# Fine weight parts on GpSimd at the ends of products, last products tile by tile, second norms in another order

## What is computed

```python
def layer(x, xc, ...):                       # first block, l = 0, 1
    h = modulate(x, g_norm1, sh1, sc1)       # rms_norm(x) * (1 + scale) + shift
    proj = h @ w_in                          # keys, values, queries, Fourier part, gates
    ...                                      # two attentions and a Fourier mix
    x = x + gt1 * merge_branches(...)        # ends in "y @ w_o"
    x = x + gt2 * conv_ffn(modulate(x, g_norm2, sh2, sc2))   # w_up, conv, silu, "@ w_down"
    # xc, the context, the same way in layer 0 alone

def second_block(x, ...):
    for layer in range(2):
        y = mixer_ab(x) if layer == 0 else mixer_c(x)        # ends in "y @ w_out"
        x = layer_norm(DEEPNORM_ALPHA * x + y, ln_gain[layer], ln_bias[layer])
```

## Time and profile before

| | us |
|---|---|
| median of three runs | 2040.17 |
| lowest, highest | 2037.59, 2048.16 |
| the profiled execution | 2048.43 |
| its span | 2046.6 |
| TensorE busy | 1922.9 |
| VectorE busy | 1184.9 |
| ScalarE busy | 932.2 |
| GpSimd busy | 161.0 |

### The profile page before, as it was taken

How to read it: one execution, slowest core, us unless ns; L and a number is a source line. 1 busy time by engine, 2 the same in 40 slices (tenths; PEclk the granted TensorE clock), 3 DMA queues, 4 the chain that set the end, 5 groups by cost and what they waited for, 6 DMA issues and landing times.

```text
span 2046.6 us, 31430 instructions
## 1 busy us (share of the span) xinstructions
PE 1922.9 (94%) x12063; PEld 1624.1 (79%) x12063; DVE 1184.9 (58%) x1944; ACT 932.2 (46%) x1424; POOL 161.0 (8%) x173
## 2 busy tenths in 40 slices
PE   5999998899998999999998989989998999799997
PEld 2875666688887888888784779989988888699996
DVE  3426556533346555533545555677744568789987
ACT  3337444422225333321436555455533646387682
POOL 4010000000001222210000000013400000000000
PEclk9999999999998999999998999989999999899999
DMA  9225557444332233233250026645557433454342
GB/s 297 96 75 165 168 183 246 121 102 105 91 103 83 83 102 102 83 112 102 93 151 14 1 67 179 192 138 180 180 185 229 124 104 103 144 165 144 125 145 103
DMA packets 262824, 265.37 MB, mean 130 GB/s; under 512 B 6310, under 2 KB 230928, under 8 KB 262720
## 3 DMA queue, kind: packets, MB, share of 16 engines
q1 hardware_dynamic: 257856, 249.32, 39.1%
q0 software_dynamic: 4416, 13.49, 2.2%
q10 hardware_dynamic: 448, 1.12, 0.2%
HBM read 262.81 MB, written 1.10 MB: 129 GB/s over the span
## 4 chain that ended last, share of the span: by engine, by line
PE 76%; DVE 12%; ACT 6%; issue 3%; DMA 3%; SPq 0%; DVEq 0%; ACTq 0%
PE bank L476 20%; PE bank L477 20%; PE bank L478 20%; PE bank L694 4%; PE bank L710 4%; DVE weights_fine L1788 3%; PE bank L470 2%; PE bank L534 2%; PE bank L523 2%; DMA region<-in_w_mod 2%; ACT weights_coarse L1121 2%; PE bank L701 1%; DVE region L2392 1%; DMA region<-in_w_in_ab 1%; PE bank L943 0%
## 5 line engine op out<-in xcount | busy, mean ns | idle before, releaser
L1788 DVE TENSOR_TENSOR weights_fine<-region,weights_coarse 128x2048 fp32r<-128x2048 f32 (+3 forms) x187 | 431.5, 2308 | 377.4 <-ACT weights_coarse L1121 376.1
L1121 ACT CAST weights_coarse<-region 128x2048 fp32r<-128x2048 f32 (+3 forms) x187 | 358.8, 1918 | 353.6 <-PE bank L478 328.6
L476 PE MATMUL bank<-normed_coarse,weights_coarse 128*128 128x256 f32 (+1 forms) x1104 | 371.8, 337 | 9.7 <-DVE fourier_out_fine L1802 5.4
L477 PE MATMUL bank<-normed_fine,weights_coarse 128*128 128x256 f32 (+1 forms) x1104 | 370.9, 336 | 0.0
L478 PE MATMUL bank<-normed_coarse,weights_fine 128*128 128x256 f32 (+1 forms) x1104 | 370.9, 336 | 0.0
L476 PEld LDWEIGHTS bank<-normed_coarse,weights_coarse 128*128 128x128 f32 x1104 | 212.6, 193 | 31.2 <-issue 10.2
L477 PEld LDWEIGHTS bank<-normed_fine,weights_coarse 128*128 128x128 f32 x1104 | 212.6, 193 | 20.6
L478 PEld LDWEIGHTS bank<-normed_coarse,weights_fine 128*128 128x128 f32 x1104 | 212.3, 192 | 20.4
L476 PE MATMUL bank<-x_turned_coarse,weights_coarse 128*128 128x256 f32 x616 | 179.5, 291 | 11.8 <-DVE x_turned_fine L1795 5.7
L477 PE MATMUL bank<-x_turned_fine,weights_coarse 128*128 128x256 f32 x616 | 177.0, 287 | 0.0
L478 PE MATMUL bank<-x_turned_coarse,weights_fine 128*128 128x256 f32 x616 | 177.0, 287 | 0.0
(11 more groups left out here) (280 smaller groups left out, 3696.8 us busy)
## 6 DMA issues: line engine op xcount, KB each, us to landing
region<-in_w_mod SPq DMA_DIRECT2D x48, 1024.0 KB, 5.2
region<-in_w_up SPq DMA_DIRECT2D x44, 1024.0 KB, 5.1
region<-in_w_in_c SPq DMA_DIRECT2D x30, 1024.0 KB, 5.1
region<-in_w_in_ab SPq DMA_DIRECT2D x20, 1024.0 KB, 5.3
region<-in_w_in SPq DMA_DIRECT2D x32, 512.0 KB, 4.7
region<-in_w_down SPq DMA_DIRECT2D x16, 1024.0 KB, 5.0
region<-in_w_in SPq DMA_DIRECT2D x14, 1024.0 KB, 5.1
region<-in_w_in SPq DMA_DIRECT2D x16, 384.0 KB, 3.6
```

Source lines behind the costliest of these rows:

```text
L476: nc.tensor.matmul(o, sc, mc, start=first, stop=False)
L477: nc.tensor.matmul(o, sc, mf, start=False, stop=False)
L1121: nc.scalar.copy(w_co[:, p, 0:size], raw_w[:, s, 0:size]).then_inc(coarse_ready, 1)
L1788: nc.vector.tensor_tensor(w_fi[:, p, 0:size], raw_w[:, s, 0:size], w_co[:, p, 0:size].bitcast(F32), ALU.subtract).then_inc(fine_ready, 1)
```

## The change

1. **Fine part on GpSimd.** In A to E the fine part of the following chunk is made by GpSimd (`weight_fine`), in four subtractions of 512 columns, with a wait for the first three ahead of the fourth. VectorE only notes it (`fine_elsewhere`) and waits for it before its own next fine part. In F there is no following chunk.
2. **Last products tile by tile.** `out_last` does part 2 as tile 0 `held`, tile 0 `rest`, tile 1 `held`, tile 1 `rest`, and takes the weights of both halves first. VectorE's statistics and layer norm, and ScalarE's roots, follow tile by tile. The same for both layers.
3. **Second norms.** VectorE scales tiles 2 and 3 ahead of the norm of tiles 0 and 1 (A); in C the order stays. ScalarE squares tile 3 behind its half of tile 0. The coarse part of odd tiles is written by a maximum of a tile with itself instead of a copy.
4. **End of the feed-forward.** On VectorE the loop over two halves is written out, and in layer 0 the rows of tiles 0 and 1 for the next norm are made behind the additions of tiles 1 and 2 (B).
5. **Constants.** Four memsets of the second block (`up_sb`, `ones`, `resets`) move from ahead of its first `turn_x` to behind its first fine part; the three steps for `lbv` move from behind E into the input products of its first layer.

Left out here: declarations and the two places where `out_last(rest)` takes the place of `out_part(2, held)` and `out_part(2, rest)`.

```diff
@@ -971,6 +972,14 @@
+            def out_last(rest):
+                part = OUT_PARTS - 1
+                w = [split_weights(WIDE_ROWS, WIDE) for _ in range(2)]
+                for t in range(2):
+                    for half, accs in enumerate((held, rest)):
+                        end(token_rows(accs[t][:, :], y2T, WIDE_ROWS * part, t, w[half], WIDE_ROWS, WIDE, False, True))
             turn_x(lambda t, half: X_UPDATES - 1 + t)
@@ -1150,14 +1157,17 @@
+            def row_root(t, updates):
+                act.wait_ge(x_done, updates + t + 1)
+                squares_of_x([t])
+                settle()
+                roots_of_x(t, t + 1)
             def norm(l, second, nt, updates):
...
                     sqrt_table()
-                    for t in range(nt):
-                        act.wait_ge(x_done, updates - nt + t + 1)
-                        squares_of_x([t])
-                        settle()
-                        roots_of_x(t, t + 1)
+                    for t in range(min(nt, 3)):
+                        row_root(t, updates - nt)
@@ -1177,6 +1187,8 @@
                     nc.scalar.copy(hT[0][:, 0:4, t * P:(t + 1) * P], affine[:, t % 2, 0:4, :]).then_inc(h_coarse, 1)
+                    if updates and t == 0 and nt > 3:
+                        row_root(3, updates - nt)
                     if l == second == 0 and t < 2:
@@ -1593,12 +1605,11 @@
                 split(CHUNK8)
-                for _ in range(2):
-                    u.event()
-                if following:
-                    split(following)
                 for t in range(2):
-                    u.event()
+                    for half in range(2):
+                        u.event()
+                        if t and half == 0 and following:
+                            split(following)
                     seen_next(ln_root)
@@ -1612,6 +1623,8 @@
             skip(2 * B_HEADS)
+            act.wait_ge(lb_diff, 1)
+            nc.scalar.activation(lbv[:, 1, :], lbv[:, 0, :], ACT.Sigmoid).then_inc(lb_ready, 1)
             for d in range(2):
@@ -1668,8 +1681,7 @@
-            act.wait_ge(lb_diff, 1)
-            nc.scalar.activation(lbv[:, 1, :], lbv[:, 0, :], ACT.Sigmoid).then_inc(lb_ready, 1)
+            step(nc.scalar.activation(small[:, 94:95], eps[:, 0:1], ACT.Sigmoid))
             turn_x()
@@ -1780,8 +1792,19 @@
+            given = [0]
+            def fine_elsewhere(size):
+                pool_fines.append((slots[0] % RING, coarse.n % PAIRS, size, coarse.n + 1))
+                slots[0] += 1
+                given[0] = coarse.next()
             def fine(size):
+                if given[0]:
+                    dve.wait_ge(fine_ready, given[0])
+                    given[0] = 0
                 s, p = slots[0] % RING, coarse.n % PAIRS
@@ -1855,6 +1878,21 @@
                 used = []
+                if second:
+                    units = []
+                    for t in range(nt):
+                        skip()
+                        units.append(later())
+                    for t in range(nt):
+                        new = t + nt // 2
+                        if new < nt:
+                            if new >= 2:
+                                dve.wait_ge(gemm_done, units[new - 2][1])
+                            norm_begin(new, new + 1)
+                            xn_of(new)
+                        norm_out(l, t, second, used, units[t])
+                    seen[h_even].next()
+                    return
                 for t in range(nt):
@@ -1864,11 +1902,8 @@
                 norm_out(l, nt - 1, second, used)
-                if second:
-                    seen[h_even].next()
-                else:
-                    fine(CHUNK8)
-                    skip()
+                fine(CHUNK8)
+                skip()
@@ -1896,7 +1931,10 @@
                     return
-                link(nc.vector.tensor_copy(hT[0][:, 4:8, at], affine[:, t % 2, 4:8, :]))
+                if second:
+                    link(nc.vector.tensor_tensor(hT[0][:, 4:8, at], affine[:, t % 2, 4:8, :], affine[:, t % 2, 4:8, :], ALU.max))
+                else:
+                    link(nc.vector.tensor_copy(hT[0][:, 4:8, at], affine[:, t % 2, 4:8, :]))
                 seen_next(h_coarse)
@@ -2157,9 +2195,11 @@
                     u.event()
-                    fine(CHUNK8)
                     if c == 0:
+                        fine(CHUNK8)
                         dve.wait_ge(gates_loaded, 16 * GATE_LOADS[2 * l])
+                    else:
+                        fine_elsewhere(CHUNK8)
                     for t in range(items_of(l)):
@@ -2215,21 +2255,25 @@
                 parts_n = len(DOWN_ROWS)
-                with dve.Fori(0, D // WIDE) as i:
-                    u.enter(i, nt, parts_n - 1 + nt)
-                    coarse.enter(i, parts_n)
+                turn = u.turn
+                for c in range(D // WIDE):
+                    u.turn = turn
                     for part in range(parts_n):
-                        fine(AFTER_DOWN[part])
+                        if c == D // WIDE - 1 and part == parts_n - 1:
+                            fine_elsewhere(AFTER_DOWN[part])
+                        else:
+                            fine(AFTER_DOWN[part])
                         if part < parts_n - 1:
                             u.event()
-                    dve.wait_ge(gates_loaded, 16 * GATE_LOADS[2 * l + 1])
+                    if c == 0:
+                        dve.wait_ge(gates_loaded, 16 * GATE_LOADS[2 * l + 1])
                     for t in range(nt):
                         b, ps = take()
-                        add_to_x(1, t, i * WIDE, t // 2, b, ps, t)
-                    for c in (u, coarse):
-                        c.leave(D // WIDE)
-                n_x[0] += (D // WIDE - 1) * nt
-                slots[0] += parts_n * (D // WIDE - 1)
+                        add_to_x(1, t, c * WIDE, t // 2, b, ps, t)
+                        if c == D // WIDE - 1 and l < DEPTH - 1 and 1 <= t <= 2:
+                            dve.wait_ge(x_done, n_x[0] - 1)
+                            norm_begin(t - 1, t)
+                            xn_of(t - 1)
@@ -2274,7 +2318,7 @@
             for l in range(DEPTH):
-                norm(l, 0, 4, None if l else first_unit, 0 if l else 2)
+                norm(l, 0, 4, None if l else first_unit, 2)
                 project(l)
@@ -2293,17 +2337,12 @@
                 dve.wait_ge(x_done, n_x[0])
-                norm(l, 1, items_of(l), started=items_of(l) // 2)
+                norm(l, 1, items_of(l))
                 ffn_up(l)
...
-
-            nc.vector.memset(up_sb, 0.0).then_inc(up_cleared, 1)
-            step(nc.vector.memset(ones, 1.0))
-            link(nc.vector.memset(resets, 1.0))
-            step(nc.vector.memset(resets.rearrange("p (c t) -> p c t", t=CHUNK)[:, :, 0:1], 0.0))
@@ -2432,18 +2471,17 @@
                 dve.wait_ge(ln_loaded, 32 * (l + 1))
+                if following:
+                    fine_elsewhere(following)
                 for t in range(2):
...
                     out_stats(t, 0)
-                for t in range(2):
                     dve.wait_ge(gemm_done, u.event())
...
                     out_stats(t, 1)
-                    if t and following:
-                        fine(following)
                     settle()
@@ -2461,6 +2499,12 @@
             chunk(units=1)
+            nc.vector.memset(up_sb, 0.0).then_inc(up_cleared, 1)
+            step(nc.vector.memset(ones, 1.0))
+            link(nc.vector.memset(resets, 1.0))
+            step(nc.vector.memset(resets.rearrange("p (c t) -> p c t", t=CHUNK)[:, :, 0:1], 0.0))
+            nc.vector.tensor_tensor(lbv[:, 0, :], cols[:, 4, T_LB + C_HEADS:T_LB + 2 * C_HEADS], cols[:, 4, T_LB:T_LB + C_HEADS],
+                                    ALU.subtract).then_inc(lb_diff, 1)
             for _ in range(6):
@@ -2540,10 +2586,6 @@
-            nc.vector.tensor_tensor(lbv[:, 0, :], cols[:, 4, T_LB + C_HEADS:T_LB + 2 * C_HEADS], cols[:, 4, T_LB:T_LB + C_HEADS],
-                                    ALU.subtract).then_inc(lb_diff, 1)
-            dve.wait_ge(lb_ready, 1)
-            link(nc.vector.tensor_scalar(lbv[:, 2, :], lbv[:, 1, :], -1.0, 1.0, ALU.mult, ALU.add))
             turn_x()
@@ -2648,6 +2690,26 @@
+            given = iter(pool_fines)
+            pieces = [0]
+            def weight_fine():
+                s, p, size, n = next(given)
+                pool.wait_ge(coarse_ready, n)
+                pool.wait_ge(fine_ready, n - 1)
+                quarter = size // 4
+                for j in range(4):
+                    at = slice(j * quarter, (j + 1) * quarter)
+                    if j == 3:
+                        pool.wait_ge(pool_piece, pieces[0])
+                    m = nc.gpsimd.tensor_tensor(w_fi[:, p, at], raw_w[:, s, at], w_co[:, p, at].bitcast(F32), ALU.subtract)
+                    if j < 3:
+                        m.then_inc(pool_piece, 1)
```

(4 more changed lines are left out.)

11 lines of the change are left out of this document (6 added, 5 removed).

## The result

The changed kernel takes 2055.47 us (median of 8 runs, 2053.31 to 2059.02), the kernel before 2040.07 (8 runs). The ratio is 1.0071, 95% interval 1.0058 to 1.0084: some 15 us slower, where I forecast 5.4, and outside my range. A second measurement gave 1.0063 (1.0041 to 1.0085).

What follows compares the result with a forecast made beforehand. TensorE, busy for 1922.9 of 2046.6 us, was taken as the bound, so the change could only win or lose in its gaps. Six places summed to 5.4 us slower: 2046 from the median of 2040.17, range 2035 to 2053.

Steps and rivals of the forecast that it cites:

- A: Output product of layer 0 to its second norm: 0.4 us gained; bounds 0.7 lost and 2.5 gained.
- E: End of the second block's first output product: 2.2 us lost; from 1.4 gained to 3.5 lost.
- F: End of the second block's last output product: 5.1 us lost, 3.4 if the clock stays.
- C: Output product of layer 1 to its second norm: 0.6 us lost; bounds 1.0 lost and 0.5 gained.
- B: End of the feed-forward of layer 0: 0.6 us gained; bounds 0 and 1.6.
- D: End of the feed-forward of layer 1: 1.5 us gained; bounds 1.0 lost and 3.3 gained.
- the critical one: Weight transfer of 11.28 us behind D, on which TensorE's later wait of 1.46 us hangs; forecast to start 2 us earlier.
- too short to lose the clock: In D, the idle before the first product, forecast to start at 1542.7 instead of 1545.99, would not lose the clock.
- landing near 1557: Sign to look for in the profile after: the transfer behind D lands near 1557.
- The port: GpSimd's pieces and VectorE's SBUF work exclude each other: about 0.6 us per instruction there, two to four a place.
- Rival 2: VectorE loses a whole 1.29 us piece at each of some 12 instructions under GpSimd: 15.5 us, so 2056; chance 0.14.
- unhindered gain of 2.5: In A, without collisions, TensorE restarts its feed-forward product at 639.6 instead of 642.1.

Runs made afterwards that it cites:

- `before`: The kernel before, unchanged, in its first profile (span 2046.6 us); median of 8 runs 2040.07 us, ratio 1.
- `consts_alone`: Kernel before, with only the constants set later (four memsets and the three `lbv` steps): ratio 0.9989.
- `all_vector`: Changed kernel, with all five fine parts back on VectorE at their old places, the rest of the change kept: ratio 1.0043.
- `kept_tiles`: Changed kernel, second buffer awaited before the second last product, GpSimd's fine part behind layer 1's feed-forward cut to 1024 columns, bias and norm rows spread: 2034.8 us.
- `first_block`: Kernel before, with the change at A, B and C alone; D, E, F and constants as before: ratio 1.0011.
- `last_alone`: Kernel before, with the last products tile by tile alone, all fine parts on VectorE: ratio 1.0038.

## Why the prediction was wrong

By place, means of the changed kernel's two profiles against the profiles that have the old code at that place:

| | forecast | measured |
|---|---|---|
| A | +0.4 | -0.4 |
| B | +0.6 | +0.8 |
| C | -0.6 | -0.2 |
| D | +1.5 | -4.7 |
| E | -2.2 | -2.4 |
| F | -5.1 | -4.9 |
| sum | -5.4 | -11.8 |

**The step that failed is D's.** It makes 6.2 of the 6.4 us between the two sums. I wrote that the transfer ahead of the critical one "starts 4 us later into the same busy stretch; the critical one starts 2 us earlier, behind it", and took 1.5 us gained, 1.0 lost at worst. The starts were right; what I kept from the trace of before was the duration of 11.28 us, and that was not a constant, nor did the busy stretch stay where it was. In both profiles the chunk ahead goes first, the rows' 3.26 MB behind it (1543.2 to 1554.5 before, 1542.6 to 1554.2 after), and the critical chunk is through only 4.8 (before) and 3.2 us behind the rows. But GpSimd now sends the rows 2.4 us behind the last addition, because they are queued behind its fine part, and the chunk ahead waits for the slot; against the same copy at the start of D the rows begin 3.5 us later than before. So the critical transfer, sent for 2.3 us earlier, takes 15.79 us and lands 2.3 us later. On top of that a longer idle stretch lost the clock, which 1.46 us had kept: it was at half from 1559.6 to 1566.4, with TensorE at work for 4.7 us of that. Against `before` D is 4.3 us longer: 2.3 by the landing and 2 by the clock. I priced the early start at TensorE but not that it only brings TensorE sooner to the same transfer. `consts_alone` shows that part by itself: its first product starts 1.7 us sooner, and TensorE then waits 2.80 us for the chunk.

Two more readings of D need a word. The idle ahead of the first product was not "too short to lose the clock": it was 1.78 us, TensorE had been busy for only 2.15 of the four us before 1538, and the clock fell to half at 1539.1, for 3.4 us, as it had in the kernel before; the sum did not rest on it. And my sign "landing near 1557" came true (1557.42) by luck: this profile runs 4.1 us ahead of the one of before, and on that one's times the landing is 1561.5.

**E and F** held to 0.2 us, for the reason given: a wait of 4.46 us for the second buffer, and its clock. I did not see that it could be taken one product later for nothing.

**The port** was sized about right: where an instruction met a piece and waited, it took 0.3 to 1.0 us more, and the row that met GpSimd's norm part of 2.35 us in A 2.1 us more. Rival 2 (12 x 1.29 us, 2056) gave the measured time, but by another cause: `all_vector` takes every piece away, and only D gets shorter. In A the 2.1 us of that row are what my +0.4 had taken off an unhindered gain of 2.5. The first feed-forward product starts 0.4 us later than before (22.8 us behind the place's first copy instead of 22.4), not 0.4 earlier; what takes these 0.8 us no run isolates.

**What stays open.** The places sum to 11.8 us, the two measurements to 14.5 and 12.9, with intervals that begin at 11.8 and 8.4. What lies between them is not placed. "B to C" and the mixer, where half-clock stretches come and go in unchanged code, are large enough for it: the first runs from +1.2 to -7.3, the second from -0.1 to +8.2. Whether the changed kernel makes them likelier in the mixer (both its profiles +5.8; `kept_tiles` too, but `first_block`, whose second block is the old one, -0.1, and `last_alone` +4.3) these runs don't settle. C is less sure than the table looks: the twelve profiles with its new code read 0.0 to +2.0, 1.0 in the mean, so the two of the changed kernel may be low.
